# High and low halves of the rows of h, t and the FFN product at a step of two

## The reference

```
h = rmsnorm(x, norm_mix)
u, b, c, (q, k, v) x 3, gate_a, gate_b = split(h @ w_in)            # 2048 -> 11776
A = (b * causal_conv3(c * u)) @ w_conv_out                           # 1024 -> 2048
B = merge(attention(q_g, k_g, v_g) for three dilated windows) @ w_attn_out   # 512 -> 2048
x = x + (sigmoid(gate_a) * A + sigmoid(gate_b) * B) @ w_out          # t @ w_out, 2048 -> 2048
h = rmsnorm(x, norm_ffn)
up, gate = split(h @ w_ffn_in)                                       # 2048 -> 2 x 5632
x = x + (silu(causal_conv3(gate) + bias) * up) @ w_ffn_down          # f @ w_ffn_down, 5632 -> 2048
y = rmsnorm(x, norm_final)
```

## Time and profile before

| | |
|---|---|
| median of 3 runs | 1520.84 us (1519.37 to 1523.67) |
| the profiled execution | 1519.65 us |
| its span | 1518.1 us |
| PE busy | 1504.6 us, 12470 matmuls |
| DVE busy | 894.6 us |
| ACT busy | 751.2 us |
| POOL busy | 76.3 us |
| mean granted PE clock | 0.997 |

### The profile page before, as it was taken

One profiled execution on the slowest core, in us unless ns is written; L12 is line 12 of the kernel. 1 busy time (PEld: TensorE's weight loads), 2 busy tenths in 40 slices (PEclk: granted clock), 3 DMA queues, 4 the chain that ended last, 5 costly groups with the idle time before them and its releaser, 6 DMA issues.

```text
span 1518.1 us, 31603 instructions
## 1 busy us (share of the span) xinstructions
PE 1504.6 (99%) x12470; PEld 1502.2 (99%) x12470; DVE 894.6 (59%) x1058; ACT 751.2 (49%) x757; POOL 76.3 (5%) x144
## 2 busy tenths in 40 slices
PE   8999999999999999999999999999999999999997
PEld 8999999999999999999999999999999999999997
DVE  8746455656676445666666565564444656556554
ACT  7555555444556344455555444554444555445452
POOL 2000001001221000100000000000000000000000
PEclk9999999999999999999999999999999999999999
DMA  8767666556788855555677776775556666565552
GB/s 276 265 185 257 181 191 220 157 162 201 221 251 256 253 181 181 180 180 168 195 249 249 239 234 210 250 246 188 182 181 181 181 184 181 177 186 191 182 181 99
DMA packets 145304, 308.64 MB, mean 203 GB/s; under 512 B 10128, under 2 KB 10384, under 8 KB 144672
## 3 DMA queue, kind: packets, MB, share of 16 engines
q1 hardware_dynamic: 139264, 268.73, 56.6%
q0 software_dynamic: 5920, 38.12, 7.5%
HBM read 301.39 MB, written 26.38 MB: 216 GB/s over the span
## 4 chain that ended last, share of the span: by engine, by line
PE 98%; DVE 1%; DMA 0%; ACT 0%; SPq 0%; DVEq 0%; issue 0%; ACTq 0%
PE acc L1000 32%; PE acc L999 32%; PE acc L998 32%; PE side L1091 1%; PE side L1070 1%; DMA raw<-w_in 0%; DVE w_split L601 0%; DVE yg L975 0%; PE side L1082 0%; PE side L1143 0%; ACT w_split L377 0%; PE side L1057 0%; PE side L1197 0%; DVE tf L851 0%; DVE tf L855 0%; ACT t_hi L506 0%
## 5 line engine op out<-in xcount | busy, mean ns | idle before, releaser
L377 ACT ACTIVATE w_split<-raw 128x1024 fp32r<-128x1024 f32 x503 | 595.3, 1190 | 664.4 <-PE acc L1000 621.4
L601 DVE TENSOR_TENSOR w_split<-raw,w_split 128x1024 fp32r<-128x1024 f32 x503 | 616.2, 1234 | 516.5 <-ACT w_split L377 511.1
L1000 PE MATMUL acc<-h_rows,w_split 128*128 128x264 f32 x2872 | 820.7, 286 | 0.0
L998 PE MATMUL acc<-h_rows,w_split 128*128 128x264 f32 x2872 | 817.1, 284 | 1.9 <-DVE w_split L601 1.9
L999 PE MATMUL acc<-h_rows,w_split 128*128 128x264 f32 x2872 | 817.8, 285 | 0.0
L998 PEld LDWEIGHTS acc<-h_rows,w_split 128*128 128x128 f32 x2872 | 555.2, 193 | 2.9 <-issue 2.3
L1000 PEld LDWEIGHTS acc<-h_rows,w_split 128*128 128x128 f32 x2872 | 557.8, 194 | 0.0
L999 PEld LDWEIGHTS acc<-h_rows,w_split 128*128 128x128 f32 x2872 | 556.5, 194 | 0.1
L1000 PE MATMUL acc<-f_rows,w_split 128*128 128x264 f32 x704 | 201.0, 286 | 0.0
L999 PE MATMUL acc<-f_rows,w_split 128*128 128x264 f32 x704 | 200.3, 284 | 0.0
L998 PE MATMUL acc<-f_rows,w_split 128*128 128x264 f32 x704 | 199.2, 283 | 0.0
(11 more groups left out here) (195 smaller groups left out, 873.4 us busy)
## 6 DMA issues: line engine op xcount, KB each, us to landing
raw<-w_in SPq DMA_DIRECT2D x183, 512.0 KB, 3.9
raw<-w_ffn_in SPq DMA_DIRECT2D x176, 512.0 KB, 4.5
raw<-w_ffn_down SPq DMA_DIRECT2D x88, 512.0 KB, 3.7
raw<-w_out SPq DMA_DIRECT2D x32, 512.0 KB, 4.2
s_kv<-cache POOLq DMA_DIRECT2D x16, 1020.0 KB, 9.1
raw<-w_conv_out SPq DMA_DIRECT2D x16, 512.0 KB, 4.7
raw<-w_attn_out SPq DMA_DIRECT2D x8, 512.0 KB, 3.6
s_kv<-cache POOLq DMA_DIRECT2D x8, 508.0 KB, 4.9
```

Of the source, the lines that this page charges most:

```text
L377: act.activation(w_hi[:, s % RING], raw[:, s % RING], ACT.Copy).then_inc(hi_ready, 1)
L601: dve.tensor_tensor(w_lo[:, s % RING], raw[:, s % RING], w_hi[:, s % RING].bitcast(F32), ALU.subtract).then_inc(lo_ready, 1)
L998: pe.matmul(out, w_hi[:, slot, k, cols], backwards(m_hi[:, kt + k, :]), start=first and k == 0, stop=False)
L1000: mm = pe.matmul(out, w_lo[:, slot, k, cols], backwards(m_hi[:, kt + k, :]), start=False, stop=last and k == 1)
```

## The change

The constant ROW_PAIR goes. `place_rows` now allocates one tensor with the two halves as its last dimension, without the padding and without the chosen start, and returns the views with index 0 and 1 of that dimension. So an element of the high half is followed by the same element of the low half, and each half is read and written at a step of two elements (8 bytes). t is placed in the same manner. ab and att stay as they were. All code that uses the views is unchanged, and every engine issues the same instructions in the same order, with other addresses and steps.

```diff
-ROW_PAIR = 576
...
         def place_rows(name, n):
 
-            off = cursor[0] + (224 - cursor[0]) % 256
-            cursor[0] = off + 4 * n * ROW_PAIR
-            rows = nc.alloc_sbuf_tensor_at(name, [P, n, ROW_PAIR], F32R, offset=off)
-            return rows[:, :, 0:T], rows[:, :, T:2 * T]
+            rows = place(name, [P, n, T, 2], F32R)
+            return rows[:, :, :, 0], rows[:, :, :, 1]
...
-        t_hi = place("t_hi", [P, KT, T], F32R)
-        t_lo = place("t_lo", [P, KT, T], F32R)
+        t_hi, t_lo = place_rows("t_rows", KT)
```

## The result

The changed kernel takes 2910.69 us, the median of 4 runs (2909.17 to 2911.26), against 1520.11 us of the kernel before on the same chip: a ratio of 1.915, 95% interval 1.912 to 1.917. The forecast was 2912 us. The profiled execution is 2909.17 us with a span of 2907.6, so 1389.5 us more than the profiled one of before; the sum had said 1391.

The account below looks back on a forecast made before the run. TensorE was taken as the bound, matmuls times their 121 ns distance. 1519.65 + 1395.1 - 4.0 + 0.2 = 2911 us, and with the median 1.2 us above the profiled run 2912 us; range 1516 to 3010 us.

Parts of the forecast that it names:

- What bounds the kernel, and the count: TensorE: the time is the number of matmuls times their distance, 121 ns; 11,520 matmuls get the new step.
- part 2: TensorE's waits of 1.9 and 0.5 us go, and about 16 half-clock matmuls cost 1.6 us less: together -4.0 us.
- Part 1: TensorE's moving reads of h, f and t at a step of two: 242 ns a matmul, +121.1 each, +1395.1 us.
- a ceiling in bytes of range: TensorE's moving read passes over at most 8.7 B/ns of one operand's address range, so 2112 B take 242 ns; chance 0.52.
- one element for each tick of 1.2 GHz, 220 ns: Neighbouring estimate for TensorE's moving reads at a step of two: 220 ns a matmul, +1140 us.
- Part 3: ACT's writes of h_hi, t_hi and f_hi at a step of two: 4.4 us, mostly hidden, +0.2 us in the open.
- Part 4: DVE's reads of hi and writes of lo: under 0.4 us, hidden; POOL's t_lo, 0 to double its 2.5 us, hidden.
- Part 5: Buffers behind h move by a few kB, t and f lose their padding: 0 us.
- Nothing: Rival: moving reads stay at 121 ns at a step of two, 1521 to 1522 us; chance 0.23.
- faster: Rival: part of the 11 ns surplus a matmul goes, 1498 us for 2 ns, 1394 for all; chance 0.15.
- A part of it: Rival: TensorE stalls by ACT's ratio 1.00/0.82, 148 ns a matmul, +311 us, 1830 us; chance 0.10.

Follow-up runs that it names:

- the half clock run: Kernel before with t at a step of two, ab and att at a step of eight, TensorE idling ahead of w_out until t is ready: 1680.2 us.

## Why the prediction was right, and where its reason was not

*What bounds the kernel, and the count.* Right. PE's distance is the time, and 11,520 matmuls changed theirs. 11,520 x 120.9 ns (242.1 less 121.2) = 1393 us, less what part 2 gives back, against 1389.5 measured.

*Part 1, the size.* Right, 242 ns as forecast. *Part 1, the reason.* Wrong, and so the number owes part of its accuracy to luck. "Nobody in this profile covers more than 8.7 B/ns" was true of that profile, and I made a ceiling in bytes of range of it. The steps of four and eight (17 and 37 B/ns) refute it. What the runs show in its place: the moving read delivers about one element each 0.917 ns (242.1/264; 0.94 at a step of four, 0.86 at eight), at a step of two at either array clock, when the elements stand alone or in pairs, and two in that time when they come in runs of four, eight or more (0.459 ns, with 512 columns as well). That the cost of a strided row is one for each element is worked out from rows of 264 columns alone; no strided row of another length was run, nor one with contiguous weights. A step of two halves both the elements in a range and, by this rule, the speed; the two theories coincide at exactly the step that the change uses. I had the second one as a neighbour, "one element for each tick of 1.2 GHz, 220 ns", and left off that the tenth of surplus, which contiguous rows already showed at full clock, goes on top: 220 x 1.1 = 242.

*Which argument of the prediction carried.* That the surplus shows only where the moving read is fastest. I took it for the sign of a limit by the read and not by the array, and the forecast stands on doubling it. For the step of two the half clock run shows such a limit; for contiguous rows it fits (0.459 is half of 0.917) and is not shown. ACT's 1.00 ns at a step of two carried less: ACT is slowed by 0.1 to 0.18 ns an element, PE by 0.46.

*The rule of the Trainium skill.* By the Trainium skill, "SBUF — State Buffer", section "Door 1: The DMA port swizzle", two hits on a line of 16 bytes are enough for full bandwidth. The moving read does not obey it: pairs and the step of two have two elements in each 16 bytes, and stand at 241.5 and 242 ns. DVE (1261 ns for f_lo, 1259 before) and the weight load (117 against 112 ns) agree with it roughly, ACT (1190 against 1057) less, and the double that all three pay at a step of four also does. The rule was right to be a rival; in this kernel it fails for the moving read and holds about for the others.

*Part 2.* Right in kind: the waits of 1.9 and 0.5 us are gone. In the kernel before, the granted clock fell to 0.50 just after PE had been idle for 1.9 us; in after PE is not idle there, the clock stays at 1.00, and all early matmuls are some 240 ns apart. Idle time alone does not foretell it, as it stayed at 1.00 through the 4.7 us of the kernel with WARM_UP = 1. The -1.6 us hold, since those 16 matmuls go from 220 to 242 ns and not from 121.

*Part 3.* Hidden, as said, but smaller than said: t_hi 1222 ns on average and f_hi 1186 instead of the 1260 forecast, h_hi 546 instead of about 550. The 1.00 ns an element was taken from the weights' copies, and in the changed kernel those too fall from 1190 to 1157 ns; that PE loads weights less densely there may be the reason, but no run tries it. The 0.2 us for the t_hi ahead of w_out do not show, as PE no longer waits there.

*Part 4.* Right: f_lo 1261 ns, POOL's t_lo 2493 ns, against 2503 before.

*Part 5.* Nearly right: rows that begin off a multiple of 32 bytes cost 2 to 4 ns a matmul, which would be visible, but `place` starts every buffer at such a multiple and a row of h, t or f in after has 2112 bytes, 66 times 32.

*The rivals.* "Nothing" (0.23) and "faster" (0.15) are out by the 242 ns. "A part of it" (0.10) had ACT's ratio as its price, 148 ns, and no stretch shows that. The low end of the range was held open for them.

What stays open: why the surplus is a tenth of the streaming time, why it falls to 3% at a step of eight (226.5 over 220), why reading forwards saves 4 ns, and why contiguous weights make the matmuls of h and f 1.7 ns slower.

## What to carry to other kernels

When a kernel is bound by matmuls, work out from start to start how many ns a column takes, at both clocks if the trace has them; a surplus that only the faster one shows is a reason to suspect the read of the moving rows, and a change of their layout will be multiplied with every matmul. Keep float32r moving rows in contiguous runs (four elements were enough here, two were not); a step of two was fine for the weights, for DVE and nearly for ACT, but that one operand bears a step says nothing of another. When two theories give the same number for the case at hand, a fitting result confirms neither: take a step at which they part.

## What the runs showed that I had not expected

- A row at a step of two takes 242 ns at half clock (0.50) and at full clock (1.00).
- For the moving read a step of eight elements (225 to 227 ns) is quicker than one of two (242) or four (247).
- Pairs of neighbours gain nothing (241.5 ns), groups of four nearly everything (125.5).
- Weights at a step of four make the whole kernel 1.9 times as long (2875 us) with contiguous moving rows, and contiguous weights are 1.1% slower than those at a step of two, nearly all of it in the matmuls of h and f.
